# Forty-eight modulation sums on ScalarE, redistributed over three stages of a transformer block

## The reference, cut to what matters

```
silu_c, silu_cc = silu(c), silu(c_ctx)
for l in range(2):
    mod_x = silu_c  @ w_ada[l] + b_ada[l]       # 6 * 1024 values
    mod_c = silu_cc @ w_ada[l] + b_ada[l]
    ...
    h = modulate(rms_norm(x, g_norm1[l]), sh1, sc1)   # h * (1 + scale) + shift
    x = x + gt1 * (attention(h @ w_in[l]) @ w_out[l])
    h = modulate(rms_norm(x, g_norm2[l]), sh2, sc2)
    x = x + gt2 * conv_ffn(h, w_up[l], conv, w_down[l])
```

## Time and profile before

| what | value |
|---|---|
| median of 3 runs | 2470.73 us (2468.18 to 2471.03) |
| the profiled execution: device time | 2474.26 us |
| its span in the trace | 2472.5 us |
| mean granted TensorE clock | 0.975 |
| out, up and down of layer 0, from the first to the last of them | about 295 to 747 us of the span |
| GpSimd products with `weights_a` (out and up) | 50 instructions, 139.6 us |
| GpSimd products with `weights_b` (down) | 46 instructions, 120.6 us |
| ScalarE activations that sum, out and up / down | 100 / 92 instructions |

### The profile page before, as it was taken

The page is one execution under the profiler, slowest core; times in us unless marked ns, Lnnn a source line. Parts: engine busy times, 40 slices in busy tenths (PEclk is TensorE's granted clock), DMA queues, the critical chain, the costliest instruction groups (busy, mean ns, idle before and its releaser), DMA issues.

```text
span 2472.5 us, 46933 instructions
## 1 busy us (share of the span) xinstructions
PE 2346.7 (95%) x17349; PEld 2129.3 (86%) x17349; DVE 1530.2 (62%) x2405; ACT 1316.3 (53%) x2439; POOL 408.2 (17%) x348
## 2 busy tenths in 40 slices
PE   7999989999887999999999999999999999998998
PEld 5786768888665878999999888999999998898998
DVE  5436586666555555885665774676556647666764
ACT  4536556665555464655444646454454445555553
POOL 1214465652882031000000000000000000000000
PEclk9999989999998999999999999999999998999999
DMA  7750133434443302556555432445545563344654
GB/s 298 225 171 10 35 127 133 145 139 121 143 152 116 95 26 81 176 173 183 168 173 170 146 107 99 154 162 178 174 134 188 168 183 107 103 156 143 194 178 130
DMA packets 101200, 356.43 MB, mean 144 GB/s; under 512 B 11344, under 2 KB 13040, under 8 KB 101072
## 3 DMA queue, kind: packets, MB, share of 16 engines
q1 hardware_dynamic: 86704, 304.45, 38.2%
q0 software_dynamic: 14368, 50.24, 6.2%
HBM read 352.55 MB, written 1.05 MB: 143 GB/s over the span
## 4 chain that ended last, share of the span: by engine, by line
PE 76%; DVE 9%; POOL 5%; issue 4%; ACT 4%; DMA 1%; DVEq 1%; ACTq 0%; SPq 0%; POOLq 0%
PE ps L783 19%; PE ps L785 19%; PE ps L784 19%; POOL products_b L744 4%; DVE wl L1796 3%; PE ps L800 2%; PE ps L801 2%; PE ps L804 2%; PE ps L923 2%; PE ps L938 2%; PE ps L909 2%; ACT wh L1321 1%; DMA ada_raw<-in_w_ada 1%; PE ps L845 1%; DVE conv L2387 1%
## 5 line engine op out<-in xcount | busy, mean ns | idle before, releaser
L1796 DVE TENSOR_TENSOR wl<-raw,wh 128x1024 fp32r<-128x1024 f32 x574 | 773.5, 1349 | 560.7 <-ACT wh L1321 559.6
L783 PE MATMUL ps<-hH,wh 128*128 128x272 f32 (+2 forms) x2864 | 886.3, 309 | 9.5 <-DVE silu L2435 3.1
L784 PE MATMUL ps<-hL,wh 128*128 128x272 f32 (+2 forms) x2864 | 872.1, 305 | 0.0
L785 PE MATMUL ps<-hH,wl 128*128 128x272 f32 (+2 forms) x2864 | 871.9, 304 | 0.0
L1321 ACT ACTIVATE wh<-raw 128x1024 fp32r<-128x1024 f32 x574 | 602.3, 1052 | 256.9 <-PE ps L785 231.8
L783 PEld LDWEIGHTS ps<-hH,wh 128*128 128x128 f32 x2864 | 543.2, 190 | 41.6 <-issue 8.3
L784 PEld LDWEIGHTS ps<-hL,wh 128*128 128x128 f32 x2864 | 543.3, 190 | 19.9 <-issue 0.5
L785 PEld LDWEIGHTS ps<-hH,wl 128*128 128x128 f32 x2864 | 543.4, 190 | 19.0
L783 PE MATMUL ps<-actH,wh 128*128 128x272 f32 (+2 forms) x1136 | 347.9, 306 | 20.0 <-DVE wl L1796 19.0
L785 PE MATMUL ps<-actH,wl 128*128 128x272 f32 (+2 forms) x1136 | 347.3, 306 | 0.0
L784 PE MATMUL ps<-actL,wh 128*128 128x272 f32 (+2 forms) x1136 | 346.2, 305 | 0.0
(11 more groups left out here) (308 smaller groups left out, 3224.0 us busy)
## 6 DMA issues: line engine op xcount, KB each, us to landing
raw<-in_w_ffn_gu SPq DMA_DIRECT2D x176, 512.0 KB, 3.5
raw<-in_w_mix SPq DMA_DIRECT2D x98, 512.0 KB, 3.5
raw<-in_w_up SPq DMA_DIRECT2D x88, 512.0 KB, 3.5
raw<-in_w_ffn_down SPq DMA_DIRECT2D x64, 512.0 KB, 3.5
ada_rest<-in_w_ada POOLq DMA_DIRECT2D x32, 512.0 KB, 4.6
raw<-in_w_out SPq DMA_DIRECT2D x32, 512.0 KB, 3.4
raw<-in_w_down SPq DMA_DIRECT2D x32, 512.0 KB, 3.5
raw<-in_w_qk SPq DMA_DIRECT2D x26, 512.0 KB, 4.3
```

What stands on the lines that cost most here:

```text
L783: pe.matmul(out, a_h, b_h, start=start, stop=False)
L784: pe.matmul(out, a_h, b_l, start=False, stop=False)
L785: return pe.matmul(out, a_l, b_h, start=False, stop=stop)
L1796: dve.tensor_tensor(wl[:, slot, :], raw[:, slot, :], wh[:, slot, :].bitcast(F32), ALU.subtract).then_inc(l_split, 1)
```

## The change

The 48 sums are given out as 3, 28 and 17. In the out stage they stand at steps 2, 4 and 6. In the up stage the first four steps have one each, and after that the second, third and fourth step of every four, up to step 35, the same last step as before; the call has moved out of the branch for the second chunk of a pair, so at even steps it comes right behind the first tap (L1696). In the down stage they stand at the first two of every three steps, and at step 2. The products, their order, their buffers and GpSimd's code stay.

```diff
-SUM_OUT, SUM_UP = 7, 18
-SUM_EARLY = SUM_OUT + SUM_UP
+SUM_OUT, SUM_UP = 3, 18
+SUM_EARLY = SUM_OUT + 3 * SUM_UP // 2 + 1
+SUM_DOWN = [j for j in range(24) if j % 3 < 2 or j == 2]
...
-                    if l == 0 and s.j:
-                        sum_products(s.j - 1, products_a)
+                    if l == 0 and s.j in (2, 4, 6):
+                        sum_products(s.j // 2 - 1, products_a)
...
-                        if l == 0 and not (isinstance(pair, int) and pair >= SUM_UP):
-                            sum_products(pair + SUM_OUT, products_a)
+                    if l == 0 and not (isinstance(s.j, int) and s.j >= 2 * SUM_UP) and (s.k or isinstance(s.i, int)):
+                        sum_products(s.i * 3 + (s.k + SUM_OUT), products_a)
...
-                    if l == 0 and s.j < NADA - SUM_EARLY:
-                        sum_products(SUM_EARLY + s.j, products_b)
+                    if l == 0 and s.j in SUM_DOWN:
+                        sum_products(SUM_EARLY + SUM_DOWN.index(s.j), products_b)
```

## The result

| | median us | ratio to the kernel before |
|---|---|---|
| before | 2470.93 (2468.18 to 2471.35, 5 runs) | |
| after | 2486.31 (2481.06 to 2487.24, 5 runs) | 1.0057 [1.0045, 1.0069] |

The change makes the kernel slower by 0.57%. The prediction was 2462 us within 2442 to 2480, with 0.64 on faster: the sign is wrong, and the result lies outside the range.

The account below looks back on a forecast made before the run. TensorE was taken to bound the up stage, and GpSimd's products the out and down stages. -8.7 - 21.5 - 11.1 - 1.8 + 34 = -9 us against 2470.7 gave 2462 us, range 2442 to 2480.

Parts of the forecast that it names:

- The out stage: Out stage with three sums instead of seven: shorter wait before the norm's matmul and a higher clock, -8.7 us.
- The down stage: Down stage with 17 sums instead of 23: TensorE sets the pace again, -21.5 us.
- rival 2: Up stage: the idle time is real slack and hides the added sums, no +34, 2428 us in all; chance 0.09.
- no reserve at its start: Start of the up stage: nothing absorbs the first sums, so TensorE waits 4.6 us together at chunks 5 to 7.
- the place of the collision: Up stage, second pair of a turn: the sum waits for its product, and VectorE asks 1.4 us into the next one.
- 24.3 or 26.7 us, 25.5 on average if they alternate as in the down stage: Up stage: time of a four-step turn, with VectorE's remainder between two products or behind both; TensorE needs 21.85.
- rival 3: Up stage: remainders always fall behind both products, turn 29.1 us, 2491 us in all; 0.19 including cases between it and forecast.
- At the end the last sum is ready before the last tile: End of the down stage: fold and norm follow in about 2.2 instead of 13.3 us, -11.1 us.
- -1.8 for the clock: End of the down stage: the norm's four matmuls run at the higher clock, -1.8 us.

Follow-up runs that it names:

- e6_up_before: Changed kernel with the up stage's 18 sums as in the kernel before, ten of the 48 sums left out; 2437.23 us, 0.9861 of before.
- e1: Changed kernel with the up stage's odd-step sums moved ahead of ScalarE's wait for VectorE's taps, all sums made; 2450.43 us, 0.9931 of before.
- e8: Kernel before the change with the up stage's 18 sums moved ahead of the wait for VectorE's taps; 2474.00 us in one run.
- e5: Changed kernel with the down stage's 17 sums given to earlier steps, none at steps 21 and 22; 2480.83 us, 1.0038 of before.
- e7: Changed kernel with e1's swap, plus the down stage's third-step sum ahead of the wait for the tile, none after step 20; 2441.22 us, 0.9880 of before.
- e3_half_sum: Changed kernel with each up-stage sum activation reading 128 instead of 512 elements; 2468.08 us in one run.
- e12: Changed kernel with GpSimd waiting, before the products for each turn's fourth step, until ScalarE has summed both products before; 2471.47 us, 1.0001 of before.

## Why the prediction was wrong

**Right.** The out stage, -8.9 for -8.7, the clock of the norm's four matmuls included. The down stage, -20.4 for -21.5, though in part by luck: the prediction gave GpSimd 13.4 us a tile at most and called TensorE the bound, but ScalarE's squares there are 16.3 us apart, more than TensorE's 15.4 for a tile. Only the lead that ScalarE and VectorE have over TensorE kept it from waiting for them until the last two tiles, 0.2 and 0.6 us (e6_up_before, with the same 17 sums, waits 0.6 to 1.0 us at every tile from the third on, and has 129.1 us). In the up stage the mechanism: the idle times of ScalarE and VectorE are no slack (rival 2 falls with the +43 us; e1 and e8 show the loop itself), and there is no reserve at its start (the first two waits, before chunks 5 and 6, are 1.2 and 3.3 us, for the 4.6 forecast). Even the place of the collision was right: a wait of 1.97 us for the product, a request 1.53 us into the next one.

**Wrong, first: "24.3 or 26.7 us, 25.5 on average if they alternate as in the down stage".** They never alternated. Two neighbouring remainders were taken for a coin toss, though one met a product that VectorE had held up and the other one that it had not. Where the third step's remainder asks, GpSimd has come straight from the load's issue, so every turn but the last takes the long way: 7 x (26.6 - 21.85) + 3.9 for the last + 4.5 at the start = 41.7 us for 34, and 43.2 were measured. That is the border at which rival 3 was said to decide, and its own mechanism was not the one: the remainder of the second step took 1.44 us in every turn, since GpSimd had waited for ScalarE before that product.

The Trainium skill, SBUF — State Buffer, section "Who interferes with whom", has the port between VectorE and GpSimd as an exclusive lock and issue order as what decides. That one of the two blocks the other agrees with all of these rows. The order does not: 144 of the 480 asked during the first product and were passed by the second.

**Wrong, second: "At the end the last sum is ready before the last tile, since 17 chunks at up to 6.7 us are 114 us".** That counts GpSimd's work as if it could run on. But ScalarE reaches the last two sums, at steps 21 and 22, only behind tile 6, and GpSimd may be no more than one chunk ahead. So GpSimd stood idle for 4.86 us, the last sum ended near 766, 6.4 us late for the fold, and the last tile's square with it. Of 12.9 us predicted (-11.1, and -1.8 for the clock, which stayed at 1.2 GHz) 3.3 came: 9.6 us too much. It is the mistake that the up stage's part of the prediction avoids. e5 and e7 bring the end to 2.0 us, and e7 without a price in the stage.

Together these are 9 + 9.6 = 19 us, from the predicted -9 to the measured +9.7 in the traces. The range failed with them: it took in 27.7 us for a turn, but with the end of the down stage as given, and nothing in it was for a sum that stands behind the last tile. Rival 3 put a price on the border (26.6 us) without a chance that showed it as likely.

## What to carry to other kernels

Where two in-order engines wait for one another, their idle time is not room for more work. Side work belongs ahead of a wait, not behind it: ten more sums cost the up stage 43 us with those of the odd steps behind the wait, and 13 us with them ahead of it. At a stage's end follow the chain of the last items (who may start only when whom has finished) instead of adding up the work. And two neighbouring rows that differ are a question, what was different before each of them, and not an average.

## What the hardware did that was not expected

Whether VectorE gets in between two products of GpSimd depends on how GpSimd came to the first of them. After it had been idle, waiting for ScalarE or a load, VectorE got in in 266 of 266 cases; when it came straight from the issue of a DMA, with VectorE free, in none of 144. The remainder then takes up to 4.97 us (e3_half_sum) instead of 1.2, and 0.7 us of waiting on GpSimd (e12) brings 4.28 down to 2.65.

TensorE's granted clock was 0.95 in the up stage after the change, where it had been 1.00: with waits of up to 3.3 us between the chunks it was at 1.2 GHz in five stretches, 24 us in all. No cost of it shows: the turns take 26.6 us with such a stretch and without. Where nothing else sets the pace, the work takes twice as long: the four matmuls of the norm need 3.7 us from 769.61 on, at 1.2 GHz, behind 10 us with 1.0 us of work, and 2.0 us from 340.18 on, at 2.4 GHz, behind 2 us of idling.
